# Stick-breaking sums as two fp32r passes in place of float32 matmuls

## The reference, cut to what matters

```
z = einsum('bqhd,bkhd->bhqk', q, k) * scale
past = s_idx < t_idx
log_fail = where(past, log_sigmoid(-z), 0.0)
later = cumsum(log_fail, axis=3, reverse=True) - log_fail
a = where(past, exp(log_sigmoid(z) + later), 0.0)
out = einsum('bhqk,bkhd->bqhd', a, v)
```

## Time and profile before

| | us |
|---|---|
| median of three runs | 1616.69 |
| lowest and highest | 1611.17, 1620.07 |
| the profiled execution | 1614.02 |
| its span | 1612.2 |
| PE busy in the span | 1537.8 (95%) |
| DVE busy | 1044.6 (65%) |
| ACT busy | 824.8 (51%) |
| the mean granted clock of PE | 0.982 |

### The profile page before, as it was taken

The page is one execution under the profiler, slowest core; times in us unless marked ns, Lnnn a source line. Parts: engine busy times, 40 slices in busy tenths (PEclk is TensorE's granted clock), DMA queues, the critical chain, the costliest instruction groups (busy, mean ns, idle before and its releaser), DMA issues.

```text
span 1612.2 us, 23627 instructions
## 1 busy us (share of the span) xinstructions
PE 1537.8 (95%) x9984; PEld 1379.2 (86%) x9984; DVE 1044.6 (65%) x1453; ACT 824.8 (51%) x1173; POOL 132.3 (8%) x132
## 2 busy tenths in 40 slices
PE   6989998999999899989999999899999997899997
PEld 5968898999888689889988987899878886799886
DVE  5795586788568755767865665666458557566446
ACT  4444554656454445455654465555446456455444
POOL 1182000000013900000000000000001000000000
PEclk9999999999999999999999999999999999999999
DMA  6431244545454223535454532455555541354551
GB/s 245 168 112 70 105 165 150 190 177 208 173 186 170 79 79 135 184 126 208 159 209 168 221 130 79 151 196 190 189 180 189 198 167 51 125 190 176 209 185 51
DMA packets 38297, 255.71 MB, mean 159 GB/s; under 512 B 4528, under 2 KB 5552, under 8 KB 8752
## 3 DMA queue, kind: packets, MB, share of 16 engines
q1 hardware_dynamic: 37904, 253.77, 43.3%
q10 hardware_dynamic: 288, 0.43, 0.1%
HBM read 253.14 MB, written 1.05 MB: 158 GB/s over the span
## 4 chain that ended last, share of the span: by engine, by line
PE 86%; DVE 8%; ACT 4%; POOL 1%; issue 1%; DMA 0%; ACTq 0%; DVEq 0%
PE psum L919 14%; PE psum L921 14%; PE psum L922 14%; PE psum L928 12%; PE psum L932 12%; PE psum L930 12%; PE psum L882 4%; PE psum L1056 2%; DVE w_low L1640 2%; PE psum L1025 2%; PE psum L1113 1%; ACT w_high L1260 1%; POOL stat L2113 1%; DVE stat L1800 1%; DVE head_work L1810 1%
## 5 line engine op out<-in xcount | busy, mean ns | idle before, releaser
L1640 DVE TENSOR_TENSOR w_low<-w_raw,w_high 128x1024 fp32r<-128x1024 f32 (+1 forms) x476 | 572.9, 1218 | 294.8 <-ACT w_high L1260 294.4
L1260 ACT ACTIVATE w_high<-w_raw 128x1024 fp32r<-128x1024 f32 (+1 forms) x476 | 495.6, 1050 | 365.1 <-PE psum L932 219.9
L919 PE MATMUL psum<-x_high,w_high 128*128 128x256 f32 x1600 | 463.6, 290 | 2.7 <-DVE x_low L1649 2.7
L921 PE MATMUL psum<-x_low,w_high 128*128 128x256 f32 x1600 | 457.0, 286 | 0.0
L922 PE MATMUL psum<-x_high,w_low 128*128 128x256 f32 x1600 | 456.4, 285 | 0.0
L919 PEld LDWEIGHTS psum<-x_high,w_high 128*128 128x128 f32 x1600 | 311.5, 195 | 9.3 <-issue 8.2
L921 PEld LDWEIGHTS psum<-x_low,w_high 128*128 128x128 f32 x1600 | 311.8, 195 | 0.4
L922 PEld LDWEIGHTS psum<-x_high,w_low 128*128 128x128 f32 x1600 | 311.4, 195 | 0.0
L928 PE MATMUL psum<-w_high,ff_high 128*128 128x512 f32 x256 | 99.8, 390 | 0.0
L930 PE MATMUL psum<-w_low,ff_high 128*128 128x512 f32 x256 | 99.6, 389 | 0.0
L932 PE MATMUL psum<-w_high,ff_low 128*128 128x512 f32 x256 | 99.6, 389 | 0.0
(11 more groups left out here) (257 smaller groups left out, 2506.8 us busy)
## 6 DMA issues: line engine op xcount, KB each, us to landing
w_raw<-in_weights SPq DMA_DIRECT2D x230, 1024.0 KB, 4.8
w_raw<-in_weights SPq DMA_DIRECT2D x4, 832.0 KB, 5.9
rows<-in_second_rows SPq DMA_DIRECT2D x4, 512.0 KB, 4.4
w_raw<-in_weights SPq DMA_DIRECT2D x2, 768.0 KB, 4.1
residual<-in_x SPq DMA_DIRECT2D x2, 512.0 KB, 6.6
w_raw<-in_weights SPq DMA_DIRECT2D x2, 512.0 KB, 3.8
out<-residual SPq DMA_DIRECT2D x2, 512.0 KB, 2.7
dil_masks<-in_consts SPq DMA_DIRECT2D x1, 576.0 KB, 5.6
```

Source lines behind the costliest of these rows:

```text
L919: eng.matmul(o, wh[:, j, cut], high[:, k, :], start=k == 0 and f % 2 == 0, stop=False, skip_group_check=True)
L921: eng.matmul(o, wh[:, j, cut], low[:, k, :], start=False, stop=False, skip_group_check=True)
L1260: act(self.unit_view(self.wh, u), raw, ACT.Copy).then_inc(sem("w_high"), 1)
L1640: tt(self.unit_view(self.wl, u), raw, self.unit_view(self.wh, u), ALU.subtract).then_inc(sem("w_low"), 1)
```

## The change

The fail values are split like the weights: ACT copies them to an fp32r tile `sb_fail_high` (signal `fail_high`), DVE subtracts that from fail to get `sb_fail_low` (signal `fail_low`). The two constant matrices get an fp32r copy in `sb_ones`, made once by ACT after the table load. PE then does each of the three products of a head twice, on the high and on the low part, in fp32r: twelve fp32r matmuls a pair in place of six float32 ones. There are two buffers of each part. Nothing is taken out of ACT's or DVE's steps, and the list of steps is unchanged: ACT's new copy stands in `sb_b`, where it had nothing to do before.

```diff
@@ stick_memory
+            self.sb_parts = [[part(sb(f"sb_fail_{name}{i}", 2 * NZ, F32R)) for name in ("high", "low")] for i in range(2)]
+            self.sb_ones = sb("sb_ones", 2 * P, F32R)
@@ tensor, sb_c
-                b, fail = j % 2, self.sb_fail[j % 2]
+                b, below, every = j % 2, self.sb_ones[:, 0:P], self.sb_ones[:, P:2 * P]
                 z = self.slot[b].rearrange("p (j n) -> p j n", j=2)
-                q.wait_ge(sem("fail_ready"), at("sb_b", j))
+                q.wait_ge(sem("sb_ones_ready"), 1)
+                q.wait_ge(sem("fail_low"), at("sb_b", j))
                 for i in range(2):
-                    for o, m, r in ((z[:, i, 0:SEQ], not_below, fail[:, i, 0:SEQ]),
-                                    (z[:, i, P:SEQ], ones, fail[:, i, SEQ:NZ]),
-                                    (z[:, i, SEQ:NZ], not_below, fail[:, i, SEQ:NZ])):
-                        d = eng.matmul(o, m, r, start=False, stop=True, skip_group_check=True)
+                    for fail in self.sb_parts[j % 2]:
+                        for o, m, r in ((z[:, i, 0:SEQ], below, fail[:, i, 0:SEQ]),
+                                        (z[:, i, P:SEQ], every, fail[:, i, SEQ:NZ]),
+                                        (z[:, i, SEQ:NZ], below, fail[:, i, SEQ:NZ])):
+                            d = eng.matmul(o, m, r, start=False, stop=True, skip_group_check=True)
@@ scalar
             elif kind == "sb_table":
                 eng.preload_act_table_set("natural_log_exp_and_others")
+                act(self.sb_ones[:, 0:P], self.const("not_below"), ACT.Copy)
+                act(self.sb_ones[:, P:2 * P], self.const("ones"), ACT.Copy).then_inc(sem("sb_ones_ready"), 1)
...
+            elif kind == "sb_b":
+                j, = key
+                q.wait_ge(sem("fail_ready"), at(*step))
+                if j >= 2:
+                    q.wait_ge(sem("later_summed"), at("sb_c", j - 2))
+                split_high(self.sb_parts[j % 2][0], self.sb_fail[j % 2], "fail_high")
@@ vector, sb_b
                 tt(fail, fail, neg, ALU.mult).then_inc(sem("fail_ready"), 1)
+                high, low = self.sb_parts[j % 2]
+                q.wait_ge(sem("fail_high"), at(*step))
+                tt(low, fail, high, ALU.subtract).then_inc(sem("fail_low"), 1)
```

## The result

| | before | after |
|---|---|---|
| median of the runs made beside each other, us | 1615.74 (6 runs, 1611.17 to 1620.07) | 1626.98 (6 runs, 1621.35 to 1627.80) |
| profiled execution / its span, us | 1614.02 / 1612.2 | 1627.75 / 1625.9 |
| mean granted clock | 0.982 | 0.976 |
| the stage: first `sb_a` to the last matmul of its output projection, by starts, us | 72.51 | 84.48 |
| in it: first `sb_a` to last `sb_d` (L1128, L1132), by starts, us | 55.92 | 67.88 |

The ratio after to before is 1.0062, with an interval of 1.0047 to 1.0077: 10.0 us slower, 7.6 to 12.4. The forecast was 1629 us with +12.1 in the sum. The change made the kernel slower, by about what was forecast.

What follows compares the result with a forecast made beforehand. PE was taken to bound the kernel (86% of the chain). The later last `sb_c` less one pair's cheaper matmuls gave +10.2 us, the clock 1.9: +12.1 on 1616.7 is 1628.8, predicted as 1629 us; range 1618 to 1637.

Steps and rivals of the forecast that it cites:

- circle through ten instructions: ACT's and DVE's queues, from one new copy to the next: 7.74 us a turn, against 5.87 of PE work.
- The copy and the subtract: New work a pair: ACT's copy at 0.84 us, bounds 0.37 and 1.04; DVE's subtract at 0.96, the shape of L1924.
- The first turn: Turn 1 of the stage, with two weight units and the take of the values: 8.36 us.
- The sums: PE's `sb_c` matmuls: 1.44 us a pair in place of 1.95, bounds 1.02 and 2.6; the 0.51 gained once.
- (C): Rival: fp32r matmuls of 128 columns in `sb_c` cost as much as float32; +14.3 us, 1631; chance 0.25, of the forecast's part.
- The last two turns: Turns 6 and 7, without a weight unit: 2 x (7.74 - 0.95) = 13.58 us, 6.79 each.
- is PE's `sb_c` off that cycle?: Whether PE's `sb_c` lengthens the queue cycle: claimed not, ending at 3.30 us, wanted at 4.9, 1.6 to spare.
- a little of the rest: Clock term: half speed after PE's gaps, 1.9 us for the last `sb_c` and some of other turns, within 0 to 6.
- Hidden and given back: Constants' copies at `sb_table` hidden in ACT's 0.46 us wait, else under 2 x 0.37; nothing after 992.6 returns the loss.
- (A): Rival: PE keeps setting the pace, ACT's and DVE's idle time absorbs the split; 4.1 to 7.4 us faster; chance 0.06.
- (B): Rival: the clock falls in the whole loop, PE at half speed from about 952; +17 to +25 us; chance 0.12.
- (D): Rival: the queue cycle is looser, a hop or the copy cheaper; loss 3 to 8 us, 1620 to 1625; chance 0.12.

Runs made afterwards that it cites:

- reordered kernel: The change with DVE making both halves and its small `sb_d` step moved behind the new subtract: 1613.47 us, ratio 0.9997 to the kernel before.
- kernel with the gaps filled: The change with idle matmuls (7, 4, 4 and 4) into an unused bank where PE would stand: 1625.56 us, ratio 1.0063 to the kernel before.

## Why the prediction was right, step by step

**The direction and the cause.** The step on which all rests, that ACT's copy closes a circle through ten instructions, held: the turns of 7.72 and 7.73 us for 7.74, the fifth of 8.88 for 8.88, and PE's idle time ahead of `sb_c` ended by the new subtract. The split alone has the same turns; a second copy and a second subtract cost unlike amounts; and without the hop to ACT, and DVE's small step moved, the loss is gone. So this is shown, not only argued.

**The copy and the subtract** took 0.84 and 0.96 us, the nearest rows' values. The bounds of 0.37 and 1.04 weren't needed.

**The first turn** was 8.28 for 8.36, and from the first `sb_a` to the first `sb_c` it took 7.6 us for 7.4 before, where no loss was forecast.

**The sums.** Forecast 1.44 us a pair, measured 1.42. Three matmuls (one of 256 columns, two of 128) start within 0.34 us, 0.11 each in the mean. The case (C), 0.267 us for one of 128 columns, did not come; as the working said, it would not have shown in the time of the turns. The gain against before was sized too large, though: the kernels with cheap sums and no split turn in 5.98 us, which is 0.40 less than the earlier trace rows, not 0.51. The unit of 12 matmuls was taken as 12 x 0.23 = 2.76, but from its first matmul to `sb_a` is 961.23 - 958.30 = 2.93 us in the kernel before, for the first and the last have more than 0.23 of their own. So the sums before were 1.78 us and not 1.95 (and 1.7 ns a column, not 1.9); the cheaper ones save 0.36, and the unit behind them starts 0.04 us tighter. It cost little here because only one pair's saving was in the sum: after the last `sb_c` the stage was 0.4 us shorter, for 0.51.

**The last two turns** were 7.60 and not 6.79: here the sums at half clock were on the circle, which the step "is PE's `sb_c` off that cycle?" had ruled out at full clock with 1.6 us to spare. By starts, without a weight unit, the way from the copy through ACT's queue to L1947 is 0.75 + 0.84 + 0.88 + 0.75 + 0.40 + 0.34 = 3.96 us. The way over the subtract and the sums is 0.87 + 1.02 + 1.61 = 3.50 at full clock (1.61 by the reordered kernel above) and 0.87 + 1.02 + 2.86 = 4.75 at half clock. The difference to 3.96 is the 0.8 of each turn. The working had put it differently, at the last `sb_c` and "a little of the rest", 1.9 us in all; the clock was in fact back at 1.00 before the last `sb_c` (duration 0.56 at 1000.31, 0.90 at 992.71) and its cost lay in turns 6 and 7. The size was 1.6 us by the kernel with the gaps filled, for 1.9; the place was wrong. And the size was in part luck: the 1.9 was a choice within 0 to 6, and in the kernels of this study the clock stays down for anything from 3.4 to 20 us (below). That the first gap (3.57 us) would be longer than before's 2.15 was not worked out, and it follows from the circle: the same matmuls ahead of a later DVE step.

**The sum.** +12.1 forecast. In the stage: 0.2 (first `sb_a` to first `sb_c`) + 12.2 (first to last `sb_c`, 55.54 for 43.33) - 0.4 (behind it) = +12.0. That this is within 0.1 of the sum is more than the terms deserve: they are off by -0.1 (turn 1), -0.3 (clock), +0.1 (sums) and +0.15 (ahead of the first `sb_c`), which nearly cancel. By medians +11.2, by the ratio +10.0 (7.6 to 12.4). The base was the median of three runs, 1616.69; with six it is 1615.74, which is 1 of the 2 us between 1629 and 1626.98.

**Hidden and given back.** The constants' copies were free, as said: what lies ahead of the stage is not longer than the scatter. Nothing gave the loss back behind it: 604.2 us after the stage against 603.3.

**The rivals.** (A), PE goes on setting the pace: refuted by the gap ahead of `sb_c` in nearly every turn. Its price of 4.1 to 7.4 us was wrong too (its upper end should by its own sum have been 7.8). Where PE did set the pace, the change of type was worth 2.3 us in the stage. The Trainium skill ("FP8 and Floating Point Precision", section TensorE Precision Notes) gives true FP32 four passes; by that alone 7.8 us were to be had. The traces don't agree for the group: 1.42 us for 1.78. Both kernels load weights twelve times a pair, and the loads are never closer than 0.11 us:

```profile
956.52 1.83 PEld L1113 LDWEIGHTS psum<-scratch,consts 128*128 128x128 f32 x12 [0.17 <-issue]
```
```profile
961.11 0.42 PEld L1117 LDWEIGHTS psum<-sb_fail_low,sb_ones 128*128 128x128 f32 x3
961.45 0.42 PEld L1117 LDWEIGHTS psum<-sb_fail_high,sb_ones 128*128 128x128 f32 x3
```

(First the kernel before, then the kernel after.) A float32 matmul is two records in the trace. Taken singly, they start 0.22 us apart with 256 columns and 0.11 with 128. So a float32 matmul of 128 columns costs 0.22 us, and so do the two of fp32r in its place; only those of 256 columns gain, 4 x (0.22 - 0.12) = 0.4 us a pair. (B), half clock in the whole loop: no; gaps of 1.6 us a turn left it at 1.00 through turns 2 and 3, it fell for 3.4 us in turn 4, where the circle's slack took it up, and stayed at 0.50 only from the end of turn 5 into turn 7. (D), a looser circle: no, every turn with weights is within 0.08 us.

**What stays open.** How long the clock stays down is not explained by the gap before it. Behind 2.15 us of idle it was at 0.50 for 3.4 us, read in steps of 0.5 us; behind 2.99 in the kernel with the cheap matmuls alone, for 3.4 too; behind 3.13 in the kernel with the split alone, for 3.4 again; around the gap of 3.57 in the change, for 17, from 980.5 to 997.5; around the gap of only 2.00 in the kernel with both halves on DVE, also for 17; and in the kernel with two subtracts for 20. Stretches of the split alone, then of the change:

```profile
980.00:982.00 2.00, 1.35 (x9) 0.58 (x7) 0.96 (x1) 1.94 (x3) 0.00 (x0) 0.57 0.00 0
982.00:984.00 2.00, 1.94 (x12) 1.65 (x12) 0.37 (x2) 1.56 (x3) 0.00 (x0) 1.00 0.00 0
```
```profile
982.00:984.00 2.00, 2.00 (x14) 1.32 (x12) 1.15 (x2) 0.98 (x3) 0.00 (x0) 0.50 0.00 0
984.00:986.00 2.00, 1.41 (x10) 1.01 (x7) 0.96 (x1) 1.94 (x4) 0.00 (x0) 0.50 0.00 0
...
996.00:998.00 2.00, 2.00 (x7) 1.57 (x6) 1.97 (x3) 0.84 (x1) 0.00 (x0) 0.61 0.00 0
```

Both have PE busy about as much; one is back at 1.00 by 982, the other not until 997.5. One profile of each is too little to say whether a second execution of the same kernel would do the same.

## What to carry to other kernels

Before adding an instruction to an engine that "has idle time", write down the order of both queues for one turn and follow each wait around: where a value goes out to a second engine and back, everything queued behind the two waits becomes one chain, and where it is longer than the pacing engine's work, its length, not any engine's busy share, is the new turn. If a value must be split in two, let one engine make both halves when it can, and put work that is ready behind the new instruction rather than a wait. A cheaper instruction on the pacing engine has to be priced in the turns where it paces; elsewhere it only makes the gap longer. And a step with room to spare at full clock has to be priced at half clock too, for then it can come onto the chain.

## What the runs showed of the hardware that was not expected

**An fp32r matmul of 128 columns costs about what one of 256 does.** Three of them, one of 256 columns and two of 128, start within 0.34 us, 0.11 each in the mean, where a stream of 256-column ones has 0.12 each. The Trainium skill ("TensorE: Matmul & The Clock Gate", section LDWEIGHTS (loading the stationary operand)) prices a weight load by its columns, columns / 1.2 in ns; 128 of them make 107 ns as an estimate from that page. The trace agrees at the full clock, with loads 0.11 us apart. At a granted clock of 0.50 it does not: the same three matmuls take 0.64 us there (986.45 to 987.09), 0.21 each.

**The same copy costs less on DVE.** The fp32r copy of 128x768 takes 0.84 us on ACT and 0.56 us on DVE, where a two-input operation of that shape takes 0.96.
